# Two-layer encoder trunk: the order in which the expert picks of four token blocks are made

## What is computed

```python
q = (hn @ wq).reshape(bsz, seq, PEER_HEADS, 2, PEER_KEY_DIM)
sc = jnp.einsum("bshpc,hpnc->bshpn", q, sub_keys).astype(jnp.float32)
v1, i1 = lax.top_k(sc[..., 0, :], PEER_TOPK)      # 8 heads, 128 keys a side, top 16
v2, i2 = lax.top_k(sc[..., 1, :], PEER_TOPK)
cand = (v1[..., :, None] + v2[..., None, :]).reshape(bsz, seq, PEER_HEADS, PEER_TOPK * PEER_TOPK)
top, ci = lax.top_k(cand, PEER_TOPK)
e1 = jnp.take_along_axis(i1, ci // PEER_TOPK, axis=-1)
e2 = jnp.take_along_axis(i2, ci % PEER_TOPK, axis=-1)
idx = e1 * N_KEYS + e2                             # one of 16384 experts
g = jax.nn.softmax(top, axis=-1).astype(hn.dtype)
...
a = jnp.einsum("td,ted->te", xb, u[ib])
w = gb * jax.nn.gelu(a, approximate=False)
return jnp.einsum("te,ted->td", w, v[ib])
```

## Time and profile before

| what | value |
|---|---|
| median of 3 runs | 4169.93 us (4169.29 to 4171.07) |
| the profiled execution, its own time | 4172.45 us |
| its span | 4170.6 us |
| granted TensorE clock, mean | 0.98 |
| PE busy | 3969.7 us (95%) |
| DVE busy | 2830.7 us (68%) |
| ACT busy | 1692.6 us (41%) |
| POOL busy | 1360.9 us (33%) |
| DMA | 879.42 MB, mean 211 GB/s |

### The profile page before, as it was taken

The page is one execution under the profiler, slowest core; times in us unless marked ns, Lnnn a source line. Parts: engine busy times, 40 slices in busy tenths (PEclk is TensorE's granted clock), DMA queues, the critical chain, the costliest instruction groups (busy, mean ns, idle before and its releaser), DMA issues.

```text
span 4170.6 us, 59348 instructions
## 1 busy us (share of the span) xinstructions
PE 3969.7 (95%) x19746; PEld 3403.8 (82%) x19746; DVE 2830.7 (68%) x4322; ACT 1692.6 (41%) x3102; POOL 1360.9 (33%) x898
## 2 busy tenths in 40 slices
PE   7999989989999999999999999899799999999998
PEld 5667877779999988888866678777799999888886
DVE  1684341599988977777717843416999889677786
ACT  2523123224666653333324221322256666444343
POOL 5344562411221432222243355633112124322231
PEclk9999999999999999999999999999999999999999
DMA  3112222227878999999721122312368789999995
GB/s 123 48 61 81 101 96 71 92 72 242 301 266 299 371 380 341 342 347 344 276 71 49 53 96 101 111 56 87 115 234 302 273 284 404 359 351 356 339 352 187
DMA packets 360972, 879.42 MB, mean 211 GB/s; under 512 B 27856, under 2 KB 191952, under 8 KB 353872
## 3 DMA queue, kind: packets, MB, share of 16 engines
q1 hardware_dynamic: 153360, 508.20, 34.0%
q0 software_dynamic: 73728, 268.47, 17.1%
q10 hardware_dynamic: 133696, 100.67, 8.0%
HBM read 774.47 MB, written 102.76 MB: 210 GB/s over the span
## 4 chain that ended last, share of the span: by engine, by line
PE 72%; DVE 14%; DVEq 4%; DMA 4%; issue 3%; ACT 2%; ACTq 1%; POOL 0%; SPq 0%
PE ps L1155 41%; PE ps L1440 21%; PE ps L1417 3%; DMA raw<-in_experts 2%; DMA act_e<-early_gelu 1%; DVE wlo L762 1%; DVE conv L818 1%; DVEq L780 1%; PE ps L1163 1%; DVEq L938 1%; DVE ubuf L1017 1%; DVE acc L1024 1%; PE ps L1203 1%; ACTq L486 1%; PE ps L1291 1%
## 5 line engine op out<-in xcount | busy, mean ns | idle before, releaser
L1155 PE MATMUL ps<-xhi,whi 128*128 128x384 f32 (+1 forms) x3328 | 1225.5, 368 | 95.2 <-DVE xlo L776 31.1
L1155 PE MATMUL ps<-xhi,wlo 128*128 128x384 f32 (+1 forms) x3328 | 1193.7, 359 | 0.0
L1155 PE MATMUL ps<-xlo,whi 128*128 128x384 f32 (+1 forms) x3328 | 1193.2, 359 | 0.0
L459 ACT ACTIVATE whi<-raw 128x1024 fp32r<-128x1024 f32 x610 | 639.4, 1054 | 340.4 <-PE ps L1440 264.5
L1155 PEld LDWEIGHTS ps<-xhi,whi 128*128 128x128 f32 x3328 | 632.7, 190 | 172.5 <-issue 67.1
L762 DVE TENSOR_TENSOR wlo<-raw,whi 128x1024 fp32r<-128x1024 f32 x512 | 622.1, 1219 | 139.2 <-ACT whi L459 133.8
L1155 PEld LDWEIGHTS ps<-xlo,whi 128*128 128x128 f32 x3328 | 633.5, 190 | 52.2 <-issue 5.3
L1155 PEld LDWEIGHTS ps<-xhi,wlo 128*128 128x128 f32 x3328 | 632.1, 190 | 53.0
L419 POOL DMA_INDIRECT ubuf<-in_up_rows,gidx x256 | 291.4, 1138 | 1131.5 <-DVE small L1017 926.5
L1440 PE MATMUL ps<-whi,eh 128*128 128x512 f32 x1536 | 601.8, 392 | 27.7 <-DVE el L1116 27.2
L1440 PE MATMUL ps<-wlo,eh 128*128 128x512 f32 x1536 | 600.3, 391 | 0.0
(11 more groups left out here) (200 smaller groups left out, 4796.8 us busy)
## 6 DMA issues: line engine op xcount, KB each, us to landing
raw<-in_experts SPq DMA_DIRECT2D x512, 512.0 KB
raw<-in_back SPq DMA_DIRECT2D x112, 512.0 KB
gate_table<-gbuf SPq DMA_DIRECT2D x48, 1024.0 KB
act_e<-early_gelu ACTq DMA_DIRECT2D x128, 384.0 KB
gtile<-gate_table ACTq DMA_DIRECT2D x30, 1536.0 KB, 23.4
raw<-in_front SPq DMA_DIRECT2D x64, 512.0 KB
raw<-in_gates SPq DMA_DIRECT2D x48, 512.0 KB
early_gelu<-weighted SPq DMA_DIRECT2D x128, 192.0 KB
```

The source lines that it names most:

```text
L459: A(whi[:, SLOT[s]:SLOT[s] + 1024], raw[:, SLOT[s]:SLOT[s] + 1024], ACT.Copy).then_inc(rounded[s], 1)
L1155: ins = MM(out, w[:, a:a + P], x[:, c, t0:], start=(i == 0 and n == 0), stop=(i == len(chunks) - 1 and n == 2))
```

## The change

The number of leading pairs becomes 8, and six pairs follow the last rows (its closing pair and `TRAIL` = 5 more). The lead holds block 1's 16 pick pieces alone; none lie between the lists. In the first row block each half has two pieces: in its halves 1 to 8 those of block 0, with the row numbers behind the last of them, in its halves 9 to 16 those of block 2. Block 3's stay in the second row block. Exp of block 0 is made by ScalarE behind half 9 (`k == 8`) and used by VectorE behind half 10. Gathered rows: none in the first ten halves, one in each of the next six, 24 in the second row block (1, 2, 1, 2, ...), 28 in the third, and one in each of the last six pairs; again 64. The gate table's last third is loaded in one piece behind the second of these pairs, and the other first loads with it. `SLOT_OF` and `TURN_OF` renumber the two pick buffers and the order of the Exps.

```diff
-LEAD = 12
+LEAD = 8
 BLOCK = HALVES + 1
 EARLY = PAIRS
-assert LEAD + DB * BLOCK + 1 == EARLY
-SELS_OF = (1, 1, 2)
-SEL_EARLY = sum(SELS_OF) * HALVES
+TRAIL = EARLY - LEAD - DB * BLOCK
...
+def spread(n, items):
+    return [n * (k + 1) // items - n * k // items for k in range(items)]
...
+SELS_OF = [0] * 10 + [1] * 6 + spread(24, HALVES) + spread(28, HALVES) + [1] * (TRAIL + 1)
+SEL_EARLY = sum(SELS_OF)
+FIRST_SEL = [sum(SELS_OF[:k]) for k in range(len(SELS_OF) + 1)]
+SLOT_OF = (0, 1, 1, 0)
+TURN_OF = (1, 0, 2, 3)
...
@@ ScalarE: row blocks and trailing pairs
+                        if b == 0 and k == 8:
+                            pick_weights(0)
                         if k == HALVES - 2 and b + 1 < DB:
                             pick_weights(b + 2)
...
-                    early_pair(i + HALVES)
                     if b + 1 < DB:
+                        early_pair(i + HALVES)
                         pick_turn(b + 2)
-                    else:
-                        gates_stored(L, 11)
-                        load_gates(L * 0, 0, 16, 22)
+                for k in range(TRAIL + 1):
+                    early_pair(EARLY - TRAIL - 1 + k, sels(DB * HALVES + k))
+                    if k == 1:
                         gates_stored(L, 12)
-                        load_gates(L * 0, 0, 22, 24)
+                        load_gates(L * 0, 0, 16, 24)
                         load_acts(L * 0, 0)
                         load_gates(L * 0, 1)
                         load_acts(L * 0, 1)
-                        early_pair(i + HALVES + 1)
...
@@ VectorE: lists
-                    if 4 <= l < 12:
-                        pick(0, l - 4)
...
@@ VectorE: lead
-                for t, k in [(0, k) for k in range(LISTS // 2, HALVES)] + [(1, k) for k in range(HALVES)]:
-                    pick(t, k)
...
+                for k in range(HALVES):
+                    pick(1, k)
...
+                    if (k + 1) * (LEAD - 2) // HALVES > k * (LEAD - 2) // HALVES:
+                        low(2 * ((k + 1) * (LEAD - 2) // HALVES + 1))
+                        low(2 * ((k + 1) * (LEAD - 2) // HALVES + 1) + 1)
...
@@ VectorE: row blocks and trailing pairs
+                PIECES = ([(0, k) for k in range(HALVES)] + [(2, k) for k in range(HALVES)], [(3, k) for k in range(HALVES)], [])
...
-                        if b + 1 < DB:
-                            pick(b + 2, k)
-                        else:
-                            drain()
+                        old = new
+                        n = len(PIECES[b]) // HALVES
+                        for t, p in PIECES[b][n * k:n * (k + 1)]:
+                            pick(t, p)
+                            if (t, p) == (0, HALVES - 1):
+                                row_numbers()
+                        if b == 0 and k == 9:
+                            pick_shares(0, gsel[:, :])
+                        drain()
...
+                for k in range(TRAIL + 1):
+                    i = EARLY - TRAIL - 1 + k
+                    new = range(FIRST_SEL[DB * HALVES + k], FIRST_SEL[DB * HALVES + k + 1])
+                    low(2 * i)
+                    for x in new:
+                        dot(x)
+                    low(2 * i + 1)
+                    axpys(old)
+                    old = new
+                    drain()
```

More of the change, by code:

```diff
@@ L64 @@
 HALVES = 2 * GROUPS
-LEAD = 12
+LEAD = 8
 BLOCK = HALVES + 1
 EARLY = PAIRS
-assert LEAD + DB * BLOCK + 1 == EARLY
-SELS_OF = (1, 1, 2)
-SEL_EARLY = sum(SELS_OF) * HALVES
+TRAIL = EARLY - LEAD - DB * BLOCK
+assert LEAD % 2 == 0 and TRAIL > 0
+def spread(n, items):
[5 more added lines that the diff above has]
+TURN_OF = (1, 0, 2, 3)
 GB = 4
@@ L355, in _ @@
                     b, k = divmod(i - LEAD - 3, BLOCK)
-                    if i >= LEAD + 3 and k < HALVES and k % 2 == 0:
+                    if i >= LEAD + 3 and b < DB and k < HALVES and k % 2 == 0:
                         store_gates(b * GROUPS + k // 2)
@@ L435, in _ @@
                 old = range(0)
-                for count in [n for n in SELS_OF for _ in range(HALVES)] + [(SEL - SEL_EARLY) // PAIRS] * PAIRS + [0]:
+                for count in SELS_OF + [(SEL - SEL_EARLY) // PAIRS] * PAIRS + [0]:
                     new = range(old.stop, old.stop + count)
@@ L686, in _ @@
                     shares(b, 0)
-                    for _ in range(SELS_OF[b]):
+                    for e in sels(b * HALVES):
                         coef(e)
-                        e += 1
                     for k in range(HALVES):
-                        new = range(e, e + SELS_OF[b]) if k + 1 < HALVES else range(e, e)
-                        early_pair(i + k, new)
-                        e = new.stop
+                        early_pair(i + k, sels(b * HALVES + k + 1) if k + 1 < HALVES else ())
                         row_copies(b, k)
@@ L935, in pick @@
                 def pick(t, k):
-                    picks = picks2[t % 2]
+                    picks = picks2[SLOT_OF[t]]
                     drain()
@@ L1066, in axpys @@
                         axpy(x)
-                e, old = 0, range(0)
+                PIECES = ([(0, k) for k in range(HALVES)] + [(2, k) for k in range(HALVES)], [(3, k) for k in range(HALVES)], [])
+                old = range(0)
                 for b in range(DB):
@@ L1077, in _ @@
                         onehots(b, k)
-                        new = range(e, e + SELS_OF[b])
+                        new = range(FIRST_SEL[b * HALVES + k], FIRST_SEL[b * HALVES + k + 1])
                         for x in new:
@@ L1083, in _ @@
                         axpys(old)
-                        old, e = new, new.stop
-                        if b + 1 < DB:
-                            pick(b + 2, k)
-                        else:
-                            drain()
+                        old = new
[6 more added lines that the diff above has]
+                            pick_shares(0, gsel[:, :])
+                        drain()
                     if b + 1 < DB:
-                        drain()
                         pick_gaps(b + 2)
-                    low(2 * (i + HALVES))
-                    low(2 * (i + HALVES) + 1)
-                    if b + 1 < DB:
+                        low(2 * (i + HALVES))
+                        low(2 * (i + HALVES) + 1)
                         pick_shares(b + 2, eidx[:, 2, :]).then_inc(pick_ready, 1)
-                for m in range(2):
-                    low(2 * (EARLY - 1) + m)
+                for k in range(TRAIL + 1):
[7 more added lines that the diff above has]
+                    old = new
+                    drain()
+                e = SEL_EARLY
                 def by_group(x):
@@ L1421, in _ @@
                         turn(b + 2)
-                early_pair(EARLY - 1, 1, EARLY // 2 - 1)
+                for i in range(EARLY - TRAIL, EARLY):
+                    early_pair(i, i % 2, i // 2)
                 pe.wait_ge(g_copied, (L + 1) * (DB * P // 4))
```

41 lines of the change are left out of this document (18 added, 23 removed).

## The result

| | before | after |
|---|---|---|
| median of the runs compared | 4169.93 us (5 runs, 4166.65 to 4174.08) | 4195.86 us (5 runs, 4192.32 to 4198.93) |
| ratio, 95% interval | | 1.0062 (1.0050 to 1.0073) |
| the profiled execution: its time, its span | 4172.45, 4170.6 us | 4198.93, 4197.1 us |
| granted TensorE clock, mean | 0.98 | 0.98 |
| PE, DVE, ACT, POOL busy | 3969.7, 2830.7, 1692.6, 1360.9 us | 3979.4, 2831.6, 1691.0, 1365.3 us |

Slower, as forecast, and inside the range; but by 25.9 us where 14.2 were forecast. No engine has more work: VectorE's busy time differs by 0.9 us, and TensorE's 9.7 more are spread over the same 19746 matmul records. What changed is where the work lies.

What follows compares the result with a forecast made beforehand. TensorE's pace was taken to bound the row blocks, VectorE nearly as busy. Losses of 53.0 us a layer against 45.9 add 14.2 for two layers to 4172.45; the run median lies 2.5 lower, so 4184 us, range 4156 to 4205.

Steps and rivals of the forecast that it cites:

- The signs listed: Observations named beforehand as showing the forecast right, or wrong: row block 2 under 183 us, clock 0.50 inside row blocks.
- Items 1 and 2, lists and lead: Start: lists without pick pieces done at 892.4, turn at 952; TensorE loses 12.5 us (10 to 15) against 29.2.
- Item 3, row block 1: Row block 1: two pick pieces a half and a wait for Exp; 14 us lost, between 11.2 and 17.
- The new wait: Row block 1: VectorE's pick_shares(0) waits for ScalarE's Exp of block 0, put at 105 us after the turn.
- Item 4, row block 2: Row block 2: VectorE needs 11.13 us a half against TensorE's 10.11; 21 us lost, between 18.9 and 24.
- Item 5: Row block 3 and six trailing pairs: TensorE sets the pace; 1.5 us lost (0 to 3.3).
- item 6: End, before the down stage: gate loads hidden, store of the last but one pair late next; 4 us lost against 11.1.
- Absorption: Rival, chance 0.25: row blocks lose at most 27 us instead of 35, fewer el waits; 8.2 less a layer, 4153.
- Nothing moves: Rival, chance 0.07: lost time only changes its place, 46 us a layer here as there; 4170.
- half-clock rival: Rival, chance 0.08: about ten idle spells a layer in the row blocks bring half clock, 8 us more a layer; 4200.

Runs made afterwards that it cites:

- no_picks_in_2: The changed kernel without the sixteen pick pieces of token block 3 in row block 2, a cause test with incomplete output: 4165.02 us, ratio 0.9982.
- rows_20_32: On top of acts_first, 20 gathered rows in row block 2 and 32 in row block 3 instead of 24 and 28: 4174.33 us, ratio 1.0000.
- lead_10: On top of acts_first, ten leading and four trailing pairs, the two rows of the pairs gone put into row block 3: 4161.41 us, ratio 0.9980.
- acts_first: The changed kernel with both gelu tile loads issued ahead of the 1.5 MB gate load instead of one behind it: 4181.38 us, ratio 1.0026.
- picks_in_lists_10: On lead_10: four block 1 pick pieces between lists, more rows beside trailing pairs, block 0's Exp earlier, first loads later: 4172.81 us, ratio 1.0008 against the kernel before.

## Why the prediction was right and where it was not

- *Direction and mechanism: right.* "The heavy part of VectorE's work is packed where TensorE's own work is dense": no_picks_in_2 shows it by taking it away (18.4 to 0.4), rows_20_32 by a part (18.4 to 7.4).
- *The signs listed.* The wait of 11.7 us behind the lists is gone, the turn comes 48 us earlier, the halves take 11 us and more, the end gap is under 5. One sign of being wrong is there too, clock 0.50 inside the row blocks; see the rivals.
- *Items 1 and 2, lists and lead: right.* 13.3 lost against 12.5; the turn at 953.60, forecast 952 (0.9 of the difference stood there before the expert stage). That eight pairs are too few there was in this number already; lead_10 cashes it.
- *Item 3, row block 1: right, a little high.* 11.7 against 14. The new wait exists, 2.41 us, and ends 104.6 us after the turn, forecast 105. The upper end of 17 by late coefficients was not needed, and the plain addition of 11.2 was closer, though the half clock found there (see the rivals) stands in none of its terms.
- *Item 4, row block 2: right, a little high.* 18.4 against 21, and the plain addition had given 18.9. A cycle of two halves takes 22.2 us in the mean (21.9 to 22.3), 11.1 each against a forecast 11.13. The rows show one half, VectorE's low part at 1209.63 and, a half on, at 1220.64:

```profile
1209.63 1.23 DVE L772 TENSOR_TENSOR wlo<-raw,whi 128x1024 fp32r<-128x1024 f32 x1
1210.78 2.35 DVE L1066 TENSOR_TENSOR onehot<-selT,const 128x1024 f32<-128x1024 f32 x2
1213.05 1.22 DVE L1026 CUSTOM_DVE_ANT_1 ubuf<-ubuf,xtok 128x1024 f32<-128x1024 f32 x1
1214.19 1.23 DVE L772 TENSOR_TENSOR wlo<-raw,whi 128x1024 fp32r<-128x1024 f32 x1
1215.33 1.28 DVE L1033 SCALAR_TENSOR_TENSOR acc<-vbuf,small,acc 128x1024 f32<-128x1024 f32 x1
1216.78 1.28 DVE L1033 SCALAR_TENSOR_TENSOR acc<-vbuf,small,acc 128x1024 f32<-128x1024 f32 x1 [0.18 <-issue]
1218.16 0.18 DVE L973 TENSOR_SCALAR rank<-pick_i 128x32 uint32<-128x32 uint32 x1
...
1220.64 1.23 DVE L772 TENSOR_TENSOR wlo<-raw,whi 128x1024 fp32r<-128x1024 f32 x1
```

- *Item 5, "TensorE sets the pace ... Lost 1.5 (0 to 3.3)": wrong, 11.5.* With it falls the sentence of item 6, "the gate loads are issued ... under four more: hidden". The load that the first step needs no longer delays the down stage, but the issues are not hidden as instructions: I counted on VectorE's 4.8 us a trailing pair and never on ScalarE, on whose queue the issues stand between two gelus. Of the 11.5, 7.2 are the wait for the held gelu and about 2.4 the half clock behind it. acts_first separates it: 2.3 once the order is changed, inside the 0 to 3.3 of the item. The trace of before had the sign. There no further up panel waited behind these issues, so their length cost TensorE no panel, but a gelu transfer behind a gate load took 3.9 us there (first row) and 12 us and more in the down stage:

```profile
1534.46 3.92 ACTq L486 DMA_DIRECT2D act_e<-early_gelu  x1
...
1670.12 12.88 ACTq L486 DMA_DIRECT2D act_e<-early_gelu  x1
...
1805.32 12.03 ACTq L486 DMA_DIRECT2D act_e<-early_gelu  x1
```

- *Item 6, end: right.* 3.3 against 4, and what is late next is the store of the last but one pair's gelus, as forecast:

```profile
1552.28 0.96 DVE L1131 TENSOR_TENSOR weighted<-act_e,gtile 128x768 f32<-128x768 f32 x1 [6.11 <-DMA early_gelu<-weighted]
```

- *The rivals.* Absorption needed row block 2 under 183 us; it took 188.5. "Nothing moves" is 0.6% off. The half-clock rival's 8 us a layer did not come, but half clock did, once a layer in row block 1. Behind a wait of 2.35 us and some matmuls at full speed ten took 0.52 us instead of 0.33:

```profile
1121.98 0.41 PE L1177 MATMUL ps<-xhi,whi 128*128 128x384 f32 x1 [2.35 <-DVE wlo L772]
```
```profile
1123.50:1126.50 3.00, 3.00 (x11) 3.00 (x11) 3.00 (x5) 1.15 (x4) 0.48 (x1) 0.50 0.43 162
```

  That is about 1.5 us, for which the prediction took no price. It seems to have cost nothing in the end: in no_picks_in_2, whose row block 1 is the same, a wait of 2.39 us at that place was followed by full speed, TensorE then waited 2.53 us instead of 1.33 for the next early gelu, and the row block lost 11.7 as well. In row block 2 TensorE stood idle about 1.3 us in every second half (the row at 1205.43 is one), and the granted clock stayed at 1.00. By the rule cited ahead from the Trainium skill, "TensorE: Matmul & The Clock Gate", section "A second HAM failure mode: psum-queue depth-cycling", short idle spells between groups would have made it swing; the trace agrees with that once in row block 1, and disagrees for the spells of row block 2.
- *The size.* Item 5's error of 10.0 a layer explains more than all of the miss: the other terms were together 4.8 too high (58.2 - 53.0 = 10.0 - 4.8). The first down matmul is 15.6 us late by the 12.3 of the table, by 2.4 of half clock that lay behind that matmul before, and by 0.9 that stood there before the expert stage began. The first down stage then gives back 6.8: the half clock's 2.4, and 2.9 of waits for el (3.8 us of them are left behind its first matmul, where there were 6.7); the rest is open. The 3.0 that the second down stage takes were not looked into, nor 2.3 us between the first down stage and the second layer's token transposes, which the change does not touch.

## What to carry to other kernels

When work moves from a stage where the matrix engine is idle to one where it is busy, add up the other engine's work per turn of the loop there against the matrix engine's pace: here 11.13 against 10.11 gave row block 2's loss within 3 us. A DMA that is issued from a computing engine's queue is an instruction of that engine: look in the trace at how long the same issue, behind the same kind of large load, holds it, and put what is on the critical path ahead of it. And look at the DMA engines of the stage that is to take the work: here a down stage at 94% and 335 GB/s reached only 96% and 346 with 16 rows more, and took 40 us longer, with VectorE a fifth idle.

## What the runs showed of the hardware that was not expected

- The issue of a transfer of gelus (384 KB) on ScalarE's queue took mostly 0.37 to 0.39 us, but 4.7 to 12.9 us fifteen times in the first down stage of the kernel before, where a gate load of 1.5 MB is issued once in four steps, and 12.55 once ahead of it in the changed kernel. Two behind a load of 0.5 MB took 6.16 together. What fixes the length was not tried.
- TensorE idled 3.33 us ahead of the first down matmul of the changed kernel, and the clock was 1.00 behind it; behind 2.56 us in rows_20_32 it was 0.50 from 1516 to 1519, and 2.36 us at 1097.26 and 2.35 at 1121.98 in the changed kernel differ in the same way. The length of one idle spell alone did not decide it.
- The DMA engines at 95 to 99% moved 346 GB/s in the down stage and 377 to 385 in row block 3.
- One addition of candidate sums (`cand`) takes 0.43 us in the earlier trace rows. Beside a subtraction of GpSimd that had begun just before, it took 2.3 and ended with it. The kernel before, between its lists, VectorE's and then GpSimd's timeline:

```profile
828.44 2.29 DVE L943 TENSOR_TENSOR cand<-vals 128x256 f32<-128x256 f32 x1
```
```profile
828.05 2.39 POOL L388 TENSOR_TENSOR wlo<-raw,whi 128x1024 fp32r<-128x1024 f32 x1 [3.97 <-ACT whi L459]
```

picks_in_lists_10 has the same pair at 835.57 (2.23 us) and 835.12 (2.40). The Trainium skill, "SBUF — State Buffer", section "Who interferes with whom", tells of such an exclusion between a VectorE operation with both inputs in SBUF and a GpSimd instruction that reads SBUF; the traces agree. Pick pieces between lists can be dearer than their own length by that. It may be a second reason why bringing them back there won nothing, but that is not shown.
